# Two stage openings with the second unit's first products moved ahead of the first unit's last ones

## The reference

```python
# end of the first block, start of the second
x = x + jnp.square(jax.nn.relu(h2 @ w_ff1[l])) @ w_ff2[l]
return rmsnorm(x, final_norm_g)
...
h = rms_norm(x, attn_norm[i])
q, k, v = jnp.split(jnp.einsum('bsd,de->bse', h, w_in), 3, axis=-1)
...
# last feed-forward part of the second block
x = x + mix
x = x + swiglu_ffn(rms_norm(x, ffn_norm[i]), w_gate[i], w_up[i], w_down[i])

def swiglu_ffn(h, w_gate, w_up, w_down):
    g = jnp.einsum('bsd,df->bsf', h, w_gate)
    u = jnp.einsum('bsd,df->bsf', h, w_up)
    return jnp.einsum('bsf,fd->bsd', jax.nn.silu(g) * u, w_down)
```

## Time and profile before

| | |
|---|---|
| median of 3 runs | 2243.19 us (2242.12 to 2243.57) |
| profiled execution, its time | 2241.81 us |
| its span, first to last instruction | 2240.1 us |
| TensorE (PE) busy | 2209.8 us, 99% of the span |
| VectorE (DVE) busy | 1201.5 us, 54% |
| ScalarE (ACT) busy | 935.8 us, 42% |
| GpSimd (POOL) busy | 219.7 us, 10% |
| TensorE clock granted, mean | 1.000 |

### The profile page before, as it was taken

How to read it: one execution, slowest core, us unless ns; L and a number is a source line. 1 busy time by engine, 2 the same in 40 slices (tenths; PEclk the granted TensorE clock), 3 DMA queues, 4 the chain that set the end, 5 groups by cost and what they waited for, 6 DMA issues and landing times.

```text
span 2240.1 us, 26887 instructions
## 1 busy us (share of the span) xinstructions
PE 2209.8 (99%) x10484; PEld 1727.7 (77%) x10484; DVE 1201.5 (54%) x1827; ACT 935.8 (42%) x1561; POOL 219.7 (10%) x312
## 2 busy tenths in 40 slices
PE   8999999999999999999999999999999999999999
PEld 6768888678888888877565888888886657888887
DVE  4574564564444444564444555554546685555454
ACT  4464334554432322334545433333335564333332
POOL 0000221211200000121323100000210001000000
PEclk9999999999999999999999999999999999999999
DMA  5212112114222232222111233322222112323233
GB/s 174 78 54 89 44 35 84 50 48 137 96 96 94 94 104 94 95 86 75 38 48 38 85 102 97 103 94 95 94 95 66 54 41 75 104 94 96 93 99 108
DMA packets 52110, 187.48 MB, mean 84 GB/s; under 512 B 5904, under 2 KB 6032, under 8 KB 51856
## 3 DMA queue, kind: packets, MB, share of 16 engines
q1 hardware_dynamic: 51984, 185.76, 25.4%
HBM read 183.64 MB, written 2.10 MB: 83 GB/s over the span
## 4 chain that ended last, share of the span: by engine, by line
PE 93%; DVE 3%; ACT 3%; issue 1%; DMA 0%; SPq 0%; ACTq 0%; DVEq 0%
PE ps L936 22%; PE ps L939 22%; PE ps L942 22%; PE ps L960 4%; PE ps L963 4%; PE ps L961 4%; PE ps L923 2%; PE ps L1283 2%; PE ps L1134 1%; PE ps L1167 1%; PE ps L1023 1%; PE ps L1271 1%; PE ps L1259 1%; PE ps L1287 1%; PE ps L1047 1%
## 5 line engine op out<-in xcount | busy, mean ns | idle before, releaser
L1335 ACT CAST wh<-raw 128x1024 fp32r<-128x1024 f32 (+1 forms) x336 | 352.9, 1050 | 869.6 <-PE ps L942 783.2
L1669 DVE TENSOR_TENSOR wl<-raw,wh 128x1024 fp32r<-128x1024 f32 (+1 forms) x336 | 416.4, 1239 | 175.5 <-ACT wh L1335 174.5
L936 PE MATMUL ps<-hh,wh 128*128 128x512 f32 x1408 | 450.9, 401 | 13.3 <-ACT hh L1351 11.9
L939 PE MATMUL ps<-hh,wl 128*128 128x512 f32 x1408 | 436.0, 391 | 0.4 <-DVE wl L1669 0.4
L942 PE MATMUL ps<-hl,wh 128*128 128x512 f32 x1408 | 435.2, 390 | 0.6 <-DVE hl L1748 0.6
L936 PEld LDWEIGHTS ps<-hh,wh 128*128 128x128 f32 x1408 | 258.7, 189 | 69.7 <-ACT wh L1335 10.2
L942 PEld LDWEIGHTS ps<-hl,wh 128*128 128x128 f32 x1408 | 264.8, 188 | 57.4 <-DVE hl L1748 1.0
L939 PEld LDWEIGHTS ps<-hh,wl 128*128 128x128 f32 x1408 | 264.5, 188 | 57.7 <-DVE wl L1669 1.8
L936 PE MATMUL ps<-R,wh 128*128 128x512 f32 x896 | 287.0, 401 | 0.0
L939 PE MATMUL ps<-R,wl 128*128 128x512 f32 x896 | 277.5, 390 | 2.4 <-DVE wl L1669 2.4
L942 PE MATMUL ps<-R,wh 128*128 128x512 f32 x896 | 276.7, 389 | 0.0
(11 more groups left out here) (225 smaller groups left out, 2193.1 us busy)
## 6 DMA issues: line engine op xcount, KB each, us to landing
raw<-in_weights SPq DMA_DIRECT2D x332, 512.0 KB, 3.3
x<-in_x_t SPq DMA_DIRECT2D x4, 512.0 KB, 7.1
F<-in_x_t SPq DMA_DIRECT2D x4, 512.0 KB, 4.4
out<-x SPq DMA_DIRECT2D x8, 256.0 KB, 2.0
raw<-in_weights SPq DMA_DIRECT2D x4, 416.0 KB, 3.2
x<-in_bias SPq DMA_DIRECT2D x1, 1024.0 KB, 6.4
C<-in_consts SPq DMA_DIRECT2D x1, 832.0 KB, 6.4
F<-in_weights SPq DMA_DIRECT2D x2, 384.0 KB, 3.6
```

The lines of the kernel that those rows point to most:

```text
L936: pe.matmul(out, hi[:, k, cs], B.tile(u.src, k)[0], start=k == 0, stop=False)
L939: pe.matmul(out, lo[:, k, cs], B.tile(u.src, k)[0], start=False, stop=False)
L1335: act.copy(B.wh[s][:, 0:nk * ncol], B.raw[s][:, 0:nk * ncol]).then_inc(S["w_hi"], 1)
L1669: dve.tensor_tensor(lo, src, hi.bitcast(F32), ALU.subtract).then_inc(S[name], 1)
```

## The change

`dense` gets an argument `crossed`. The pieces of all units of a stage are first put into one list, and then walked through; with `crossed` true the first entries of that list are put into another order. The two stages named above are called with `crossed` true. For all others the list of steps stays the same.

```diff
-    def dense(self, units, more=None):
+    def dense(self, units, more=None, crossed=False):
 
-        n = 0
+        n, order = 0, []
         for u in units:
-            self.place(u)
...
+            order += [(u, piece) for piece in pieces]
+        if crossed:
+            order = order[:3] + order[4:6] + order[3:4] + order[6:]
+        for u, piece in order:
+            self.place(u)
+            tick, extra = self.low() + self.due(), (more or {}).get(n, [])
+            n += 1
+            if u.kind == "rows" and piece[2] % u.nk == 0:
+                steps = self.ready(u, piece[2] // u.nk - 1)
+                tick += steps[:-1] + extra + steps[-1:]
+            else:
+                tick += extra
...
+            yield [("mm", u, *piece)], tick
...
-        self.run(self.dense(uq[0] + uk[0], roots(2, True)))
+        self.run(self.dense(uq[0] + uk[0], roots(2, True), True))
...
-        self.run(self.dense(chain(ff2b), roots(5)))
+        self.run(self.dense(chain(ff2b), roots(5), True))
```

More of the change, by code:

```diff
@@ L349, in dense @@
                 pieces = [(i, a, a + 2) for i in range(4) for a in range(0, 8, 2)]
[L350 to L364, removed]
+            order += [(u, piece) for piece in pieces]
[10 more added lines that the diff above has]
+                tick += extra
+            if u.kind == "cols" and piece[2] == 8:
+                if piece[0] == 3:
+                    tick.append(("ev", u))
+                    if u.ev == "dq":
+                        self.heads(u)
+                tick += self.split(u.chunks[piece[0]] + 2)
+            yield [("mm", u, *piece)], tick
         rest = self.due(True)
```

## The result

The changed kernel takes 2249.99 us (median of 7 runs, 2248.75 to 2250.77) against 2242.22 us for the kernel before (7 runs beside it, 2241.78 to 2243.59). That is +7.8 us, a ratio of 1.0033 with a 95% interval from 1.0024 to 1.0042. Forecast were +5.1 us and 2248.3 us, with a range to 2250.0 us: the direction and the three waits came as written, and 2.7 us came on top that the sum did not contain. The profiled execution has 2250.55 us and a span of 2248.8 us, 8.7 more than before.

The account below looks back on a forecast made before the run. TensorE, busy for 2209.8 of 2240.1 us, was taken as the bound. The terms 1.82 + 1.67 + 1.60 gave +5.09 us, so a median of 2248.3 us, with an 8 in 10 range of 2245.9 to 2250.0 us.

Parts of the forecast that it names:

- the three waits: TensorE waits for wl: +1.82 us at the first opening, +1.67 at the second, +1.60 at the second's u2p0.
- part a: At both openings the fourth tick becomes u1p0 and waits for wl of c1: +1.82 and +1.67 us.
- part b: Split of c2 and u0's eviction move to the sixth tick: +1.60 us at the second opening's u2p0, nothing at the first.
- Nothing is given back: Behind the openings the loss stays, as TensorE's list is fixed and it has nothing else to overtake.
- The clock: Granted clock stays 1.00, nothing in the sum; a fall at the first opening would cost up to 2.8 us, chance 0.07.
- the rival's 2251.1: Clock falls in the first opening's stall, TensorE starts the stage at 1.2 GHz: up to 2251.1 us, chance 0.07.
- the likeliest case: Forecast as summed over both openings: +5.09 us, own range +4.0 to +6.2 us, chance 0.70.

Follow-up runs that it names:

- the first experiment: The new order at the first opening only, the second opening put back to the old order, against the changed kernel: 2246.61 us, ratio 1.0017 to the kernel before.

## Why the prediction was right or wrong

**Where the new fourth tick waits** (part a): right at both openings and to a few hundredths: 968.48 against 968.16 + 0.32, 1885.27 against 1881.50 + 3.77. The order on VectorE decides it, and the run with that order turned round shows it: from the last x tile to the products with wl it is 2.37 us instead of 4.37 at the first opening, and 2.38 instead of 3.41 at the second.

**The wait at u2p0** (part b): right in size, 1.60 us by the sum (1897.62 against the shifted 1892.66, less 3.36 us that had come before). What the prediction left out is that it can't be taken away by one early subtraction; it moves on to u3. At the first opening, where I costed it at nothing, the trace shows none.

**Nothing is given back**: right. The shift of 3.7 us behind the first opening is there in full 900 us later.

**The clock**: the step that failed. The prediction put its cost at nothing in the sum ("The granted clock stays 1.00"), priced a fall at up to 2.8 us for the first opening alone, gave it 0.07, and argued that the clock had been held over a wait of 2.4 us. It came true at both openings, +1.50 and +1.69 us, and with it the measured 2249.99 lies nearer to the rival's 2251.1 than to the forecast's 2248.3. The argument was weak in the row it stood on: the earlier trace rows is one execution. Of the ten kernels profiled here in which that 2.4 us wait stands unchanged and unfilled, seven show a clock under 1.00 behind it. A wait that passes once without a fall says little on whether it will the next time. The size was priced fairly: 1.50, 1.69 and 2.79 us a fall at the openings, against up to 2.8.

**The range** held by 0.01 us (2249.99 in 2245.9 to 2250.0), which is luck: the +7.8 us lie outside the likeliest case's own +4.0 to +6.2. The three waits came within some hundredths of the sum of 5.09 us, and the room above them should have gone to the clock instead.

**What stays open**: why the low clock lasts some 3 us in the one kernel and nearly 7 in the other, why the unchanged wait of 2.4 us is followed by a fall in seven profiles and not in three, and whether the fall near 1845 us makes the upper group of the kernel before. Where c1's wl comes late at the second opening and nothing fills the wait, the three profiles differ with what came before: in two the clock held behind the 2.4 us wait, TensorE waited 1.88 us at the opening, and the clock fell there; in the third it fell behind the 2.4 us wait, TensorE came late, waited 1.35 us, and the clock held. Whether it is the shorter wait that saves the clock there no run tests.

## What to carry to other kernels

Work moved ahead to cover a wait needs its own operands, and they come out of the same queues: look up when each of them is made in the old trace before counting the cover. Here the wait was for the last tile, and the substitute's weights were made right behind that tile on the same engine. Where an order gives one unit's successor two ticks instead of four, the preparation chain behind it becomes the next wait, and mending it there passes it on. And a new wait of TensorE is priced with a stretch at half clock behind it: here the wait of 3.2 us was followed by one in three of three profiles, that of 2.4 us in seven of ten. Then look at what TensorE waits for next. Where TensorE's next wait is for a chain on another engine that the lost time does not hold up, the fall is made good in that wait, and filling gains nothing (2242.02 against 2242.23 us behind the 2.4 us wait). Where it is not made good, products that nobody reads are worth their trouble (2.7 us at the first opening).

## What the runs showed of the hardware that had not been expected

The clock fell while TensorE was idle (0.84 in the stretch from 966 to 968 us of the first experiment) as well as just after it had started again (0.56 from 968 to 970 us of the changed kernel), and the low level lasted some 3 us in one case and nearly 7 us in the other, behind waits of equal length (3.2 us). Behind the wait of 2.4 us it fell in seven profiles and not in three. In two of 13 profiles it fell at the end of three waits of 0.5 to 0.8 us that lie close together (0.50 from 1846 to 1848 us with the new order at the second opening only), at a cost of 1.5 us. A fall need not cost anything: behind the 2.4 us wait ahead of the second opening it takes the place of TensorE's next wait, 1.04 us for hh at 1879.58, and `stat` starts within 0.04 us of where it would have.
